# Other places, modulo 256 bytes, for the high and low weight parts that TensorE loads

## The chip, the cores and the metric

The kernel runs on one core of one Trainium2 chip. The metric is device time in microseconds (us), from start to end of one execution. An execution of the kernel before takes 3118.19 us, the median of two (3118.02 and 3118.37).

## What is computed

The reference is a block in float32 over one sequence of 256 tokens with 2048 features, followed by a second kind of block, which is applied twice. Each takes a normed input through wide projections, a few attention heads or a recurrence, gates and an output projection:

```python
h = rms_norm(x, g);  proj = h @ w_in            # 2048 x 17408, then twice 2048 x 16192
y_rnn  = (rg_lru(rnn_x) * silu(rnn_gate)) @ w_rnn_out
y_attn = (dilated_attention(q, k, v) * silu(attn_gate)) @ w_attn_out
x = x + rms_norm((sigmoid(g_rnn) * y_rnn + sigmoid(g_attn) * y_attn) @ w_o, ln_post_g)
for l in range(2):                              # three attention branches A, B, C
    u = rms_norm(x, g_pre[l]) @ w_in2[l]
    y = sum(sigmoid(gate_n) * ((branch_n * silu(z_n)) @ w_branch[l, n]) for n in "ABC")
    x = x + y @ w_out2[l]
```

Nearly all the arithmetic is multiplication of a 256-token activation matrix by weight matrices that are each used once.

## The kernel before

**Two parts of every number.** TensorE multiplies in a one-pass type (`fp32r`) that keeps fewer bits than float32. So each weight and each activation is held as a high part (a rounded copy) and a low part (what the rounding lost), and three of the four products are summed: high by high, high by low, low by high. ScalarE makes the high parts (`hi`, line 929, its instruction is line 937), VectorE the low ones (`lo`, line 1275, its instruction is line 1280), both from the buffer `raw`, into which the SyncE queue loads the weights by DMA.

**Tiles.** Weights come in units of 8 row tiles by 256 columns (128 x 2048 numbers). Units go to two slots in turn (`j % 2`). A unit is made, freed and used by halves of 1024 columns (`h`). The buffer `hl` holds, for each slot, the high parts of both halves and the low parts of both halves. `part(j, e, h, ...)` (line 218) gives the columns of slot `j`, part `e` (0 high, 1 low), half `h`. Right behind `hl` in on-chip memory lies `hT` and behind it `uT`, the activations: for each of 16 row tiles 512 columns, 256 tokens in high parts and then the same 256 in low parts. `hT` begins 4 x `HL` bytes behind the start of `hl`, and `hT` and `uT` are each 32768 bytes a partition, a multiple of 256.

**The matrix multiplications.** Every one on `pg` is issued by `mm` (line 536) and has two operands: the stationary one (128 x 128), loaded by a LDWEIGHTS ahead of it, and the moving one, which streams past. In `feature_major` (line 562) the stationary operand is a weight tile from `hl` and activations move: the wide one (512 columns) multiplies high weights by high and low activations at once, the narrow one (256 columns) low weights by high activations. They alternate, wide, narrow, wide, narrow; where `SIDE` (line 98) says so, a row tile or a half has its wide ones first and then its narrow ones. A half is 8 wide and 8 narrow ones. In `token_major` (line 570, for the values of the attentions) the roles are swapped: an activation tile is stationary, and the weights of `hl` move, high and low parts as one operand of two stretches (`both_view`, line 582). `queries` (line 803) and `keys_and_values` (line 812) issue their three products as single narrow ones. Each stationary tile starts a multiple of 512 bytes from the start of its half, and each moving one of `feature_major` a multiple of 1024 bytes from the start of `hT` or `uT`, so that within a half all have the same place modulo 256 bytes.

**Order.** TensorE's order is written out (`EVENTS`, `unit`). PSUM results are joined by ScalarE (line 945) and VectorE (line 1287). Small multiplications on `pa` for the attentions, the recurrence and the norms, most of them in plain float32, stand between the halves.

Of the kernel before, what the change touches and what calls it, by code (L numbers as in the profile page):

```python
# [26 lines left out]
UC = 2048  # L27
# [120 lines left out]
RAW_CHUNKS, RAW_HEAD = 5, 6  # L148


HI_AT, LO_AT, SLOT, HL = 16, UC + 32, 2 * UC + 128, 4 * UC + 224


PRE_SUMS = [1, 2 + NCH, 4 + 2 * NCH]
# [33 lines left out]
def build(nc, xT, w_in, w_gate, w_rnn, w_att, w_o, w_in2, w_uq, w_ukv, w_br, w_out2,  # L188
          vec1, vec2, blam, consts, tabs, bias_c, outT):
    ctx = ExitStack()  # L190
    with ctx:
        def sb(name, cols, dt=F32):
            return ctx.enter_context(nc.sbuf_tensor(name, [P, cols], dt))
# [5 lines left out]
        hl = sb("hl", HL, F32R)  # L199
# [17 lines left out]

        def part(j, e, h, a=0, n=UC // 2):

            first = j % 2 * SLOT + (LO_AT if e else HI_AT) + h * UC // 2 + a  # L220
            return hl[:, first:first + n]

        h3 = hT[:, :].rearrange("p (t n) -> p t n", n=512)
# [151 lines left out]
        def _(sp):  # L375
# [62 lines left out]
            with sp.Fori(0, PAIRS) as p:  # L438
                u = U_P1 + p * units("1")
                for part, base in enumerate((Q1, K1, V1)):  # L440
                    for g in range(3):
                        for j in range(2):
                            wide(u + 6 * part + 2 * g + j, j, w_in, base + 1024 * g + p * CH, 1024 * j)
                for j in range(2):
                    wide(u + 18 + j, j, w_in, Z1 + p * CH, 1024 * j)
                for j in range(4):
                    wide(u + 20 + j, j, w_in, G_ATT + (2 * p + j // 2) * CH, 1024 * (j % 2))
# [86 lines left out]
        def _(pe):  # L534
# [3 lines left out]
            def split_view(j, n):  # L538

                return [[part(j, e, k * n // (UC // 2), k * n % (UC // 2), n) for k in range(UC // n)] for e in range(2)]  # L540
# [37 lines left out]
            def apart_view(j, n):  # L578

                return [[part(j, e, h, 0, n) for h in range(2)] for e in range(2)]  # L580

            def both_view(j, n):
                views = []
                for k in range(UC // n):
                    h, a = k * n // (UC // 2), k * n % (UC // 2)
                    first = j % 2 * SLOT + HI_AT
                    pair = hl[:, first:first + 2 * (LO_AT - HI_AT)].rearrange("p (e n) -> p e n", e=2)
                    views.append(pair[:, :, h * UC // 2 + a:h * UC // 2 + a + n])
                return views

            def opening(u0, c0, tiles_ready, first_parts, weights_parts=None, summed=None):
# [20 lines left out]
            def unit(u, j, c, cj, op, first, last, form="f", subs=2, ready=None, halves=(0, 1), first_parts=None, side=()):  # L612

                base = 0 if first else 8
                if form == "k":
                    base, first, last = 0, True, True
                wh, wl = split_view(j, CH)
                if form == "r":
                    wh, wl = ([[w[h][:, k * P:k * P + P] for k in range(4)] for h in range(2)] for w in apart_view(j, 512))
                for h in halves:  # L620
                    pe.wait_ge(lo_done, 2 * u + h + 5)
                    if first and h == 0 and c is not None:
                        pe.wait_ge(evac_done, c + 1)
                    start, stop = first and h == 0, last and h == 1
                    parts = [range(base + 4 * h, base + 4 * h + 4)] if form != "k" or h == 0 else [(4, 5), (6, 7)]
                    if first_parts is not None and h == 0:
                        parts = first_parts
                    for n, ks in enumerate(parts):
                        if ready is not None:
                            ready(ks)  # L630
                        b, begin, end = 2 * (cj % 2), start and n == 0, stop and n == len(parts) - 1
                        if form == "r":
                            ins = feature_major(b, subs, wh[h], wl[h], op, ks, begin, end, base + 4 * h, side)
                        elif form == "t":
                            ins = token_major(b, wh, both_view(j, CH), op, ks, begin, end, base, side)
                        else:
                            ins = feature_major(b, subs, wh, wl, op, ks, begin, end, base, side)
                    ins.then_inc(half_done, 1)
# [253 lines left out]
            for l in range(2):  # L892
# [20 lines left out]
                for kind in "ABC":  # L913
                    turns = 2 if kind == "A" else 1
                    with pe.Fori(0, PAIRS // turns) as i:
                        for n in range(turns):
                            p = i * turns + n
# [1034 lines left out]
```

## Time and profile before

| | |
|---|---|
| median of the runs | 3118.19 us |
| the profiled execution's own time, its span | 3120.9 us, 3119.0 us |
| TensorE matmul busy | 3097.6 us (99%), 18230 instructions |
| TensorE weight load busy | 2731.5 us (88%) |
| VectorE, ScalarE busy | 2128.8 us (68%), 1733.3 us (56%) |
| DMA engines, mean busy share | 59.4% for the one data queue |
| granted TensorE clock | 0.998 of full speed |

The span runs from the first to the last instruction; the execution's own time also holds what lies around it. A matmul's busy time includes the flow through the array, which overlaps the next one. So the distance from one start to the next says more than the busy time: where a run of n matmuls is one row, it is (length of the row less the length of the last) / (n - 1).

### The profile page before, as it was taken

Reading aid. Unit: us, or ns where it says so; the run is one execution under the profiler, and the core shown is the slowest. Engines: PE = TensorE matmul, PEld = TensorE weight load, DVE = VectorE, ACT = ScalarE, POOL = GpSimd, SP = SyncE. Lnnn points to the kernel's source line nnn. Section 1 sums busy time; section 2 is a strip of 40 time slices with the busy share of each in tenths; the row PEclk is TensorE's granted clock in tenths of the full one; section 3 lists DMA queues with packets and bytes.
Section 4 is the critical chain, followed back from the end, with each engine's and each line's share of the span. In section 5 each row is a group of like instructions: output and inputs, shape, how many; then the busy total and the mean of one; then the engine's idle time right before and its main releaser. Section 6 shows DMA issues by size and latency. Waiting matters only on the chain.

```text
span 3119.0 us, 52176 instructions
## 1 busy us (share of the span) xinstructions
PE 3097.6 (99%) x18230; PEld 2731.5 (88%) x18230; DVE 2128.8 (68%) x2741; ACT 1733.3 (56%) x2291; POOL 0.2 (0%) x4
## 2 busy tenths in 40 slices
PE   9999999999999999999999999999999999999999
PEld 7888888888888788888888888888988888888888
DVE  7677576666667687767676565777776767656574
ACT  5685444444445556656565555645665656555563
POOL 0000000000000000000000000000000000000000
PEclk9999999999999999999999999999999999999999
DMA  7656655555556565565656665666556565666555
GB/s 228 194 176 197 205 189 167 184 180 174 183 169 211 179 174 161 160 204 171 182 167 195 192 185 176 189 197 185 160 160 205 170 182 167 195 192 186 176 187 175
DMA packets 569810, 571.67 MB, mean 183 GB/s; under 512 B 26353, under 2 KB 565489, under 8 KB 569713
## 3 DMA queue, kind: packets, MB, share of 16 engines
q1 hardware_dynamic: 569712, 570.42, 59.4%
q8 instruction: 56, 0.92, 0.1%
q14 instruction: 42, 0.34, 0.0%
HBM read 568.25 MB, written 2.10 MB: 183 GB/s over the span
## 4 chain that ended last, share of the span: by engine, by line
PE 96%; DVE 2%; ACT 1%; issue 1%; DMA 0%; SPq 0%; DVEq 0%; ACTq 0%
PE pg L536 90%; PE pa L775 1%; PE pa L792 1%; PE pa L782 1%; PE pa L536 1%; PE pa L751 1%; DVE hl L1280 1%; PE pa L793 1%; ACT hl L937 0%; PE pa L708 0%; PE pa L883 0%; DMA raw<-w_in 0%; DVE mix L1815 0%; DVE xres L1739 0%; DVE uT L1818 0%
## 5 line engine op out<-in xcount | busy, mean ns | idle before, releaser
L536 PE MATMUL pg<-hT,hl 128*128 128x512 f32 x11456 | 2001.4, 335 | 1.2 <-DVE hl L1280 1.1
L536 PEld LDWEIGHTS pg<-hT,hl 128*128 128x128 f32 x11456 | 1732.9, 188 | 235.0 <-DVE hl L1280 5.4
L1280 DVE TENSOR_TENSOR hl<-raw,hl 128x1024 fp32r<-128x1024 f32 (+1 forms) x1071 | 1255.1, 1210 | 299.6 <-ACT hl L937 291.9
L937 ACT ACTIVATE hl<-raw 128x1024 fp32r<-128x1024 f32 (+1 forms) x1071 | 1085.1, 1044 | 295.1 <-PE pg L536 277.9
L536 PE MATMUL pg<-uT,hl 128*128 128x256 f32 (+1 forms) x3712 | 631.5, 332 | 15.9 <-DVE uT L1361 7.4
L536 PEld LDWEIGHTS pg<-uT,hl 128*128 128x128 f32 x3712 | 555.8, 190 | 87.0 <-issue 15.5
L945 ACT ACTIVATE corr<-pg 128x512 f32<-128x512 f32 x286 | 170.2, 595 | 822.8 <-PE pg L536 822.8
L536 PE MATMUL pg<-hl,hT 128*128 128x512 f32 (+1 forms) x1792 | 318.5, 336 | 0.0
L536 PEld LDWEIGHTS pg<-hl,hT 128*128 128x128 f32 x1792 | 274.6, 188 | 38.6
L1287 DVE TENSOR_TENSOR work<-pg,corr 128x512 f32<-128x512 f32 (+1 forms) x154 | 105.8, 687 | 293.6 <-ACT corr L945 293.3
L1112 ACT ACTIVATE work<-work,sm 128x256 f32<-128x256 f32 (+3 forms) x144 | 69.3, 482 | 131.1 <-DVE sm L1558 129.1
L1287 DVE TENSOR_TENSOR gat<-pg,corr 128x512 f32 (+1 forms) x71 | 49.0, 690 | 133.0 <-ACT corr L945 133.0
L1287 DVE TENSOR_TENSOR xres<-pg,corr 128x512 f32<-128x512 f32 x32 | 22.1, 691 | 42.1 <-ACT corr L945 42.1
L1558 DVE TENSOR_REDUCE sm<-work 128x1 f32<-128x256 f32 (+3 forms) x144 | 49.0, 391 | 1.9
L1118 ACT ACTIVATE uT<-work 128x256 f32 x52 | 20.0, 414 | 53.2 <-DVE work L1689 53.2
L984 ACT ACTIVATE work<-pa,sm 128x256 f32<-128x256 f32 (+1 forms) x58 | 42.1, 726 | 3.4 <-PE pa L693 2.2
L1567 DVE RECIPROCAL sm<-sm 128x2 f32<-128x2 f32 (+1 forms) x56 | 9.5, 170 | 50.3 <-ACT work L1112 50.3
L1554 DVE SCALAR_TENSOR_TENSOR work<-pa,tab 128x384 f32<-128x384 f32 (+2 forms) x56 | 43.6, 779 | 0.0
L1287 DVE TENSOR_TENSOR corr<-pg,corr 128x512 f32<-128x512 f32 x15 | 10.4, 691 | 48.5 <-ACT corr L945 48.5
L792 PE MATMUL pa<-work 128*128 128x256 f32 x144 | 42.8, 378 | 0.0
L985 ACT ACTIVATE work<-work 128x256 f32<-128x256 f32 (+1 forms) x58 | 39.7, 685 | 1.8
L980 ACT ACT_TABLE_LOAD x31 | 39.8, 1283 | 1.3 <-PEq L1946 0.7
(191 smaller groups left out, 1369.1 us busy)
## 6 DMA issues: line engine op xcount, KB each, us to landing
raw<-w_in SPq DMA_DIRECT2D x791, 512.0 KB, 4.7
raw<-w_br SPq DMA_DIRECT2D x96, 512.0 KB, 4.3
raw<-w_out SPq DMA_DIRECT2D x64, 512.0 KB, 4.8
raw<-w_rnn SPq DMA_DIRECT2D x32, 512.0 KB, 4.9
raw<-w_o SPq DMA_DIRECT2D x32, 512.0 KB, 5.3
raw<-w_att SPq DMA_DIRECT2D x16, 512.0 KB, 4.7
raw<-w_uq SPq DMA_DIRECT2D x16, 384.0 KB, 3.9
tab<-tabs SPq DMA_DIRECT2D x5, 896.0 KB, 7.3
```

Of the source, the lines that this page charges most:

```text
L536: return nc.tensor.matmul(out, lhsT, rhs, start=start, stop=stop, skip_group_check=True)
L792: nc.tensor.matmul(weighted(kind, e), va, pt[:, 0:S], start=m == 0, stop=False, skip_group_check=True)
L937: nc.scalar.activation(part(j, 0, h, 0, n), raw[:, bass.ds(j % 2 * UC + a, n)], ACT.Copy)\
L945: nc.scalar.activation(cr[:, cj % 2, 0:n, :], pg3[:, b:b + n, S:], ACT.Copy)\
L980: act.preload_act_table_set("natural_log_exp_and_others")
L984: steps.done(nc.scalar.activation(out, mean, ACT.Ln, bias=eps, scale=scale))
L985: ins = nc.scalar.activation(out, out, ACT.Exp, scale=-0.5)
L1112: ins = nc.scalar.activation(part, part, ACT.Exp, bias=nmax[:, n:n + 1], accum_out=lsum[:, n:n + 1])
L1280: tt(part(j, 1, h, 0, n), raw[:, bass.ds(j % 2 * UC + a, n)], part(j, 0, h, 0, n).bitcast(F32), ALU.subtract).then_inc(lo_done, 1)
L1287: return tt(out, pg3[:, b:b + n, 0:S], cr[:, cj % 2, 0:n, :], ALU.add)
L1554: steps.done(stt(sc.rearrange("p (m n) -> p m n", m=nm), pa3[:, bank:bank + nm, 0:SM], SCALE[kind], tab[:, m0:m0 + SM * nm].rearrange("p ( ...
L1558: ins = nc.vector.tensor_reduce(nmax[:, n:n + 1], part, AX.XY if kind == "1" else AX.X, ALU.max, negate=True)
```

## The change

Four constants go (`HI_AT`, `LO_AT`, `SLOT` and the old `HL`), and a table `AT[slot][part][half]` takes their place, which gives the first column of each of the eight pieces of `hl`. Nothing else is touched: the same instructions on the same numbers, in the same order, with the same waits. Before, both halves and both slots had one place for high parts and one for low parts modulo 256 bytes; now each slot and half has a pair of its own. `hl` grows from 8416 to 8624 columns of 4 bytes, so that `hT` and all that lies behind it moves up by 832 bytes.

```diff
-HI_AT, LO_AT, SLOT, HL = 16, UC + 32, 2 * UC + 128, 4 * UC + 224
+AT = (((48, 2160), (1120, 3216)), ((4288, 6400), (5344, 7472)))
+HL = 8624
...
         def part(j, e, h, a=0, n=UC // 2):
 
-            first = j % 2 * SLOT + (LO_AT if e else HI_AT) + h * UC // 2 + a
+            first = AT[j % 2][e][h] + a
             return hl[:, first:first + n]
...
                 for k in range(UC // n):
                     h, a = k * n // (UC // 2), k * n % (UC // 2)
-                    first = j % 2 * SLOT + HI_AT
-                    pair = hl[:, first:first + 2 * (LO_AT - HI_AT)].rearrange("p (e n) -> p e n", e=2)
-                    views.append(pair[:, :, h * UC // 2 + a:h * UC // 2 + a + n])
+                    first, apart = AT[j % 2][0][h], AT[j % 2][1][h] - AT[j % 2][0][h]
+                    pair = hl[:, first:first + 2 * apart].rearrange("p (e n) -> p e n", e=2)
+                    views.append(pair[:, :, a:a + n])
                 return views
```

## Rows read from the trace of the kernel before

**Rows 1.** The page's first lines: busy time by engine, and its chain by engine.
```profile
span 3119.0 us, 52176 instructions
...
PE 3097.6 (99%) x18230; PEld 2731.5 (88%) x18230; DVE 2128.8 (68%) x2741; ACT 1733.3 (56%) x2291; POOL 0.2 (0%) x4
...
PE 96%; DVE 2%; ACT 1%; issue 1%; DMA 0%; SPq 0%; DVEq 0%; ACTq 0%
```

**Rows 2.** Waits of TensorE: engine, line, releaser, us in total, times, longest.
```profile
PE pg L536 <- DVE uT L1361: 7.4, 3, 3.7
PE pg L536 <- DVE hl L1485: 6.8, 1, 6.8
PE pg L536 <- DVE hl L1280: 1.9, 5, 0.5
```

**Rows 3.** Groups by line and shape, whole span (out<-moving,stationary): busy us, mean ns | idle us.
```profile
L536 PE MATMUL pg<-hT,hl 128*128 128x512 f32 x5728 | 1969.6, 393 | 1.2 <-DVE hl L1280 1.1
L536 PE MATMUL pg<-hT,hl 128*128 128x256 f32 x5728 | 1560.4, 277 | 0.0
L536 PE MATMUL pg<-uT,hl 128*128 128x512 f32 x1664 | 574.9, 395 | 15.9 <-DVE uT L1361 7.4 <-DVE hl L1485 6.8 <-DVE hl L1280 0.8
L536 PE MATMUL pg<-uT,hl 128*128 128x256 f32 x2048 | 504.9, 280 | 0.0
L536 PE MATMUL pg<-hl,hT 128*128 128x512 f32 x896 | 312.4, 393 | 0.0
```

**Rows 4.** Windows: stretch, its us, TensorE busy us (matmuls), granted clock, DMA share, GB/s.
```profile
251.00:442.00 191.00, 191.00 (x1126) 1.00 0.64 202
583.57:605.77 22.20, 22.20 (x130) 1.00 0.62 198
```

**Rows 5.** Timeline in four short windows, matmuls and weight loads: start us, length us.
```profile
1300.03 0.50 PE L536 MATMUL pg<-hT,hl 128*128 128x512 f32 x2
...
1300.26 0.50 PE L536 MATMUL pg<-hT,hl 128*128 128x256 f32 x2
...
1300.26 0.19 PEld L536 LDWEIGHTS pg<-hT,hl 128*128 128x128 f32 x1
...
122.16 3.61 PE L708 MATMUL pa<-xres 128*128 128x256 f32 x16
```

**Rows 6.** Timeline, runs of one kind of one-pass matmul.
```profile
246.70 1.55 PE L536 MATMUL pg<-hT,hl 128*128 128x512 f32 x6
...
248.43 1.00 PE L536 MATMUL pg<-hT,hl 128*128 128x256 f32 x7
...
1174.86 3.58 PE L536 MATMUL pg<-uT,hl 128*128 128x256 f32 x29
```

**Rows 7.** The chain that ended last, in order of time: start us, length us, what.
```profile
1715.90 0.93 PE pa L536 x4
...
1753.02 32.80 PE pg L536 x192
...
1956.64 5.48 PE pg L536 x32
```

**Rows 8.** Groups by line and shape: the two instructions that write the weight parts.
```profile
L1280 DVE TENSOR_TENSOR hl<-raw,hl 128x1024 fp32r<-128x1024 f32 x1047 | 1239.7, 1222 | 296.2 <-ACT hl L937 288.5
...
L937 ACT ACTIVATE hl<-raw 128x1024 fp32r<-128x1024 f32 x1047 | 1071.0, 1054 | 284.7 <-PE pg L536 267.5 <-DMA raw<-w_in 9.9 <-DMA raw<-w_o 3.5
```

## The prediction, made before the changed kernel was run

> **What bounds the kernel now.** I read the busy times and the chain first: TensorE's matmuls cover 99% of the span and 96% of the chain [rows 1]. The waits come next: few have a name, and the longest sums are 7.4, 6.8 and 1.9 us [rows 2]. So the time is the number of matmuls times the distance between their starts, and the change can only act on that distance. The groups by shape give the numbers [rows 3]: 5728 + 1664 = 7392 wide feature-major matmuls, each with a narrow partner (2048 - 1664 = 384 narrow ones are left, in the products of branch A), and 896 token-major pairs.
>
> The distance is in the windows [rows 4]. From 251 to 442 us nothing but alternating wide and narrow ones run, at full clock: 191.00 us for 1126 matmuls, one or two of which began before the window, so 562 pairs at 191.00 / 562 = **340 ns a pair**. That is 17/16 of 768 columns at 2.4 GHz (320 ns). The token-major stretch from 583.57 to 605.77 holds 64 pairs of its own, besides a row at each edge: 22.20 / 64 = **346.9 ns a pair**. The columns and the clock are the same. What differs is which buffer moves and which is loaded, and with it the place of the one relative to the other.
>
> **Who meets whom.** A weight load begins with a matmul: at 1300.26 both a narrow matmul and a load start [rows 5]. So while matmul i streams its moving operand, the stationary tile of matmul i+1 is being read. During a wide one low weights are loaded, during a narrow one high weights. What counts is then (place of the loaded tile - place of the moving one) modulo 256 bytes. I call it the lag.
>
> Before: high parts start at 16 x 4 = 64, low parts at 2080 x 4 = 128 (mod 256), half and slot add multiples of 256, and `hT` lies at 8416 x 4 = 128. Lags: low 0, high 64 - 128 = 192. Token-major: activations loaded at 128 while high weights move at 64, lag 64.
>
> After: `hT` lies at 8624 x 4 = 192. High parts: slot 0 at 192 in both halves, slot 1 at 0. Low parts: slot 0 at 128 and 64, slot 1 at 128 and 192. So the lags (high, low) become slot 0: (0, 192) and (0, 128); slot 1: (64, 192) and (64, 0). The change's title says (64, 0), (64, 192), (128, 0), (128, 64). Those differ from mine by 64 in both entries, because the longer `hl` moves the activations too. None is the old pair (192, 0).
>
> **The price of a lag, where the trace shows one.**
> - Wide, lag 192: the run of wide ones at 246.70, (1.55 - 0.39) / 5 = 232 ns [rows 6].
> - Wide, lag 0: four wide ones of the norm sums, moving and stationary both from `uT`, 0.93 / 4 = 232 ns [rows 7]. Lag 128 appears nowhere; between a wide one in step (2/3 of 340 = 227) and the 232 of its neighbours I take 232, the nearest rows out of step.
> - Narrow, lag 0: (1.00 - 0.28) / 6 = 120 ns, the run at 248.43 [rows 6].
> - Narrow, lag 192: from the products in threes of branch A, (3.58 - 0.28) / 28 = 118 ns on average over two loads of lag 192 and one of lag 0, so (3 x 118 - 120) / 2 = 117 [rows 6].
> - Pair with lag 64: the token-major 346.9.
>
> Added up, slot 0 would take 232 + 120 = 352 a pair and slot 1 about 347, mean 349.5. The same sum for the old places is 232 + 117 = 349, and the trace has 340: the alternating pair there falls into a rhythm in which both operands go by without loss, and lags alone don't foretell it. The lower end for each place is therefore 340, the upper end the sum. I put one of the four places in step, but with a re-entry at each half, since the lags now change every 2.7 us. What an entry costs: 32 matmuls behind small other work take 5.48 us against 16 x 0.34 = 5.44, so 40 ns, 5 ns a pair over the 8 pairs of a half [rows 7]. That place counts 345. The forecast is 0.75 x 349.5 + 0.25 x 345 = 348.4 ns.
>
> What the old kernel really has per pair in a mixed stretch: 32.80 / 96 = 341.7 ns [rows 7]. So each of the 7392 pairs pays 348.4 - 341.7 = 6.7 ns more: **+49 us**.
>
> **The other parts.** Token-major pairs: lags become 0 in slot 0 (load at 192, high weights moving at 192) and 192 in slot 1, by the prices above 352 and 349 instead of 346.9, about 3 ns x 896 = +3 us; bounds -6 us (340) and +5 us. The 384 single narrow ones read slot 0 (lags 0, and 192 or 128): at most 120 - 118 = 2 ns each, under 1 us. The writers of the parts, lines 1280 and 937, take 1.22 and 1.05 us a half [rows 8] and end inside the 2.72 us that TensorE needs for one; they cost nothing here, and without that cover a tenth more on 1047 of each would be 128 and 110 us. No slot, wait or DMA is added; a slower TensorE gives all others more time. The small multiplications on `pa` have both operands behind `hl` and keep their lags. The few stops of rows 2 stay.
>
> Sum: +49 + 3 = +52, less some because the sum of single prices overstated the old places by 9 ns, and the new ones may lie partly lower: I take **+47 us**. The profiled execution's 3120.9 becomes 3168; it stands 2.7 us over the median 3118.2, so the predicted time is **3165 us**.
>
> **A rule against this.** The rows show that the one-pass narrow matmul takes 113 to 120 ns while other operands differ in place alone. The Trainium skill says otherwise: "SBUF — State Buffer", section "Who interferes with whom", gives TensorE two independent read ports, one for the moving operand and one for LDWEIGHTS, and ends "PE and ACT never wait on anyone". By that rule places can't matter, and the time would stay 3118 us. The 340 against 346.9 of rows 4 speaks against it, though there the roles are swapped too and not the places alone; it is the first rival below.
>
> **The rivals.**
> 1. *No effect.* 17/16 may be what a one-pass stream takes whatever is loaded, and the token-major 7 ns may come from the swapped roles (two stretches in one operand). For it: 340 ns holds over 191 us without a slip. Against: single-kind runs of the same operands are slower (232 and 120, not 227 and 113). Then 3118, within 3110 to 3130.
> 2. *Slower by more, collision at every load.* If the changing lags keep TensorE from any rhythm: 232 + 120 = 352 for all, and the entry of 5 ns a pair on top, 357 - 341.7 = 15 ns x 7392 = +113 us, 3231 us. It decides from about 350 ns a pair on, where 2% is lost (62 us / 7392 = 8.4 ns a pair). For it: narrow, lag 0, is the dearest row, and all of slot 0 has it. Against: the old sum overstated.
> 3. *Faster: one place beats 17/16.* A plain float32 matmul of 256 columns has starts (3.61 - 0.38) / 15 = 215 ns apart [rows 5], near 512 columns' 213 at 2.4 GHz. If new places let one-pass ones run like this, a pair takes 215 + 108 = 323, up to 19 ns less; all four would give -138 us (2980), one of four -35 us (3083). For it: no row has lag 128. Against: no stretch in the trace, at any of three lags, goes below 340 a pair. By the Trainium skill's "TensorE: Matmul & The Clock Gate", section "Wait — 56ns, not 53.3ns?", starts are N / 2.4 GHz + 2.5 ns apart, 325 for a pair; the trace's 340 doesn't agree for this type.
> 4. *It doesn't do what it says*: if the title's pairs were the true lags (activations unmoved), slot 0 would have narrow 64 and slot 1 narrow 128, unpriced; by the sums above +30 us, inside the forecast.
>
> **How the numbers follow.** A change of 2% is 62 us, about what can be told from none. Forecast, with rival 4 in it (3130 to 3200): 0.63, of which I put 0.16 above 3181. No effect: 0.17. Slower by more: 0.14. Faster: 0.06, of which over 2% only where two places or more gain, 0.02. So slower by over 2% 0.16 + 0.14 = 0.30, faster by over 2% 0.02, within 0.68. The range takes the no-effect case and most of the forecast up to the foot of rival 2: 3114 to 3214.
>
> **What would show it.** In the changed profile the window 251:442 should hold about 1100 matmuls, not 1126, and not one stretch of 191 us in one rhythm; slot 0's halves should be longer than slot 1's, because of narrow ones of 120 ns; the runs on `pa` should keep 0.93 us for four; DVE and ACT instruction lengths and the waits should not move. Wrong would be: all halves at 2.72 us (rival 1), pairs under 340 (rival 3), or a named wait of TensorE that grew.

## The result: 3166 us, and the profile after

The changed kernel takes 3166.11 us (median of two, 3165.81 to 3166.42) against 3118.19: a ratio of 1.0152, 95% interval 1.0136 to 1.0168, **+48 us** where +47 was forecast. The page of the changed kernel (busy time by engine, chain by engine) has the same engines in the same order as [rows 1], each share within one point; TensorE's busy time has grown by 44 us with no instruction more:

```profile
span 3164.5 us, 52176 instructions
...
PE 3141.8 (99%) x18230; PEld 2751.5 (87%) x18230; DVE 2130.0 (67%) x2741; ACT 1733.0 (55%) x2291; POOL 0.2 (0%) x4
...
PE 97%; DVE 1%; ACT 1%; DMA 0%; SPq 0%; issue 0%; ACTq 0%; DVEq 0%
```

TensorE's waits (line numbers are one higher throughout) are those of [rows 2], with 2.2 us more on low parts:

```profile
PE pg L537 <- DVE uT L1362: 7.9, 3, 3.5
PE pg L537 <- DVE hl L1486: 6.7, 1, 6.7
PE pg L537 <- DVE hl L1281: 4.1, 6, 1.6
```

The writers of the parts, against [rows 8], have not moved by more than 1 ns:

```profile
L1281 DVE TENSOR_TENSOR hl<-raw,hl 128x1024 fp32r<-128x1024 f32 x1047 | 1240.4, 1221 | 315.4 <-ACT hl L938 307.9
...
L938 ACT ACTIVATE hl<-raw 128x1024 fp32r<-128x1024 f32 x1047 | 1070.2, 1053 | 307.2 <-PE pg L537 288.1 <-DMA raw<-w_in 9.7 <-DMA raw<-w_o 4.4
```

So the time is in the distance between matmuls. The two windows of [rows 4], in the changed kernel:

```profile
251.00:442.00 191.00, 191.00 (x1099) 1.00 0.61 196
583.57:605.77 22.20, 22.20 (x129) 1.00 0.60 189
```

1099 instead of 1126 in the same 191 us at the same clock. Counted as the prediction counts, less the two that may have begun before the window, these are 548.5 pairs of 191.00 / 548.5 = 348.2 ns where it was 340. (The second window begins at another point of the work.) The chain of the changed kernel in order of time (start, length, what), for [rows 7]:

```profile
1743.95 0.92 PE pa L537 x4
...
1769.13 5.54 PE pg L537 x32
...
1781.57 33.40 PE pg L537 x192
```

33.40 / 96 = 347.9 ns a pair where it was 341.7: 6.2 x 7392 = 46 of the 48 us. The four wide ones on `pa`, whose two operands moved together, stay at 0.92 us.

The 96 pairs of this row are not all of one kind: by their tiles, 80 are feature-major and the last 16 token-major. Taking 346.9 ns for each of the 16 in both, the 80 took (32.80 - 5.55) / 80 = 340.6 ns before and take (33.40 - 5.55) / 80 = 348.1 now, 7.5 ns more, and in the long window the step is 8.2 ns. At that price 7392 pairs would cost 55 to 61 us and not 48. Part of the rest is that the kernel before was not in step everywhere. A later window, in the kernel before and then in the changed one:

```profile
2000.00:2100.00 100.00, 100.00 (x574) 1.00 0.61 190
```

```profile
2000.00:2100.00 100.00, 100.00 (x576) 1.00 0.58 184
```

100.00 / 286 = 350 ns a pair before the change, at the old lags and at full clock; the changed kernel is a little quicker here. In the trace of the kernel before, 326 pairs in a row from 1995.8 us and 270 from 3020.3 us run like this.

The four places show in four halves in a row, timeline of the changed kernel. Each row runs from a half's third matmul to its fifteenth, wide at both ends, so a pair is (length - 0.395) / 6:

```profile
304.55 2.48 PE L537 MATMUL pg<-uT,hl 128*128 128x512 f32 x13
...
307.33 2.49 PE L537 MATMUL pg<-uT,hl 128*128 128x512 f32 x13
...
310.14 2.52 PE L537 MATMUL pg<-uT,hl 128*128 128x512 f32 x13
...
312.97 2.43 PE L537 MATMUL pg<-uT,hl 128*128 128x512 f32 x13
```

Slot 0 with lags (high, low) = (0, 192) takes 347 ns and with (0, 128) 349; slot 1 with (64, 192) takes 354 and with (64, 0) 339, which is in step. From the first start of a half to the first of the next, entries included, they are 347, 351, 353 and 342, mean 348.3. The mean is the forecast's, the places are not: the dearest half was to be in slot 0.

### The profile page after: what moved, and what is told of

Its sections match the earlier page's. It is cut to its first block, busy times and chain, and to the rows that moved or that the text cites. A ratio compares the mean times of both kernels' runs of the same rounds, so it can differ in the third digit from the quotient of the medians.

```text
span 3164.5 us, 52176 instructions
## 1 busy us (share of the span) xinstructions
PE 3141.8 (99%) x18230; PEld 2751.5 (87%) x18230; DVE 2130.0 (67%) x2741; ACT 1733.0 (55%) x2291; POOL 0.2 (0%) x4
## 4 chain that ended last, share of the span: by engine, by line
PE 97%; DVE 1%; ACT 1%; DMA 0%; SPq 0%; issue 0%; ACTq 0%; DVEq 0%
PE pg L537 91%; PE pa L776 1%; PE pa L793 1%; PE pa L537 1%; PE pa L783 1%; PE pa L752 1%; PE pa L794 1%; DVE hl L1281 0%; PE pa L709 0%; DMA raw<-w_o 0%; PE pa L884 0%; DMA raw<-w_in 0%; ACT hl L938 0%; SPq L456 0%; DVE uT L1362 0%
## 5 line engine op out<-in xcount | busy, mean ns | idle before, releaser
L537 PE MATMUL pg<-hT,hl 128*128 128x512 f32 x11456 | 2036.4, 338 | 2.1 <-DVE hl L1281 2.0
L537 PE MATMUL pg<-uT,hl 128*128 128x256 f32 (+1 forms) x3712 | 639.4, 334 | 16.8 <-DVE uT L1362 7.9
```

Of the source, the lines that this page charges most:

```text
L537: return nc.tensor.matmul(out, lhsT, rhs, start=start, stop=stop, skip_group_check=True)
```

## The experiments

Four theories. **L**: the lags set the distance. **A**: the absolute place in memory does, or the longer `hl`. **C**: only lags that change from half to half cost. **M**, formed after the first four kernels: L with memory, that is, the same pair of lags has more than one rhythm, and what ran before picks it. Ratios are against the kernel before, with 95% intervals.

**All lags alone, TensorE alone (grid).** The edit replaces the block by one line for each pair of lags:

```python
run((192, 0), mm)      # 64 pairs: for k in 8, s in 2: wide(k, s), narrow(k, s), four times
```

> A program of its own, in place of the block: after one load and two copies, TensorE alone runs 31 stretches of 64 wide and 64 narrow one-pass matmuls (or 64 of one kind), each stretch with a fixed pair of lags (high, low): all 16 pairs of 0, 64, 128, 192, four single wide, four single narrow, and seven with lags of 16 or 32 bytes between. Theory L (the lag of the loaded tile to the moving one sets the distance): (192, 0) takes 340 ns a pair, (64, 192) 341, (64, 0) 347, (0, 192) 350, (0, 128) 352 to 353, as in the kernels; at least one other pair reaches 340, none goes below. Rival A (the place in memory itself, or what the other engines do at the time, sets it): all 16 pairs take the same here, 340. Rival C (only the change of lags from half to half costs): all 16 settle at 340 as well.

Its chain in order of time; each line of the program is one pair of lags (high, low). L73 is (0, 128), L74 (0, 192), L75 (64, 0), L78 (64, 192), L79 (128, 0), L80 (128, 64), L83 (192, 0), L86 (192, 192); L87, L89 and L90 are wide ones only, lag 0, 128 and 192, L91 and L94 narrow ones only, lag 0 and 192:

```profile
64.85 22.19 PE pg L73 x128
87.04 22.40 PE pg L74 x128
109.44 21.78 PE pg L75 x128
...
176.22 22.59 PE pg L78 x128
198.81 22.52 PE pg L79 x128
221.33 22.19 PE pg L80 x128
...
288.17 21.76 PE pg L83 x128
...
354.31 22.61 PE pg L86 x128
376.92 14.51 PE pg L87 x64
...
406.36 14.88 PE pg L89 x64
421.24 14.65 PE pg L90 x64
435.89 7.67 PE pg L91 x64
...
458.69 7.54 PE pg L94 x64
```

Divided by 64: (64, 0) and (192, 0) take 340 ns a pair, (0, 128) and (128, 64) 347, (0, 192) 350, (128, 0) 352, (64, 192) and (192, 192) 353. Seven of the eight not shown lie between 347 and 353; (0, 0), which ran first and began with wide ones 427 ns apart and more, settles at 347. No pair goes under 340. Nothing else runs here, and the spread is that of the kernels: A and C, which had all at 340, fall. Single kinds: wide 227 at lag 0, 233 at 128, 229 at 192; narrow 120 at lag 0, 118 at 192. Of the pairs off the grid, (192, 16) also took 340 and (176, 0), (208, 0), (192, 32) 347 to 353.

**Same lags, other absolute places (shift_all).**

```diff
-HI_AT, LO_AT, SLOT, HL = 16, UC + 32, 2 * UC + 128, 4 * UC + 224
+HI_AT, LO_AT, SLOT, HL = 32, UC + 48, 2 * UC + 128, 4 * UC + 240
```

> The kernel before with weight parts and activations all 64 bytes further on, so that all lags stay (192, 0). Theory L: 3118 us, 340 ns a pair between 251 and 442 us. Rival A (the place in memory itself counts, modulo 256): off 3118 by tens of us, as the changed kernel is. Rival C: 3118.

Measured: ratio 1.0002 (0.9992 to 1.0011); the first window holds x1125. Moving every place by the same 64 bytes costs nothing that can be seen; more places of the moving tile are in grid2.

**One pair of lags everywhere (uni_64_192, uni_0_128).**

```diff
-AT = (((48, 2160), (1120, 3216)), ((4288, 6400), (5344, 7472)))
+AT = (((0, 2112), (1056, 3168)), ((4224, 6336), (5280, 7392)))      # uni_64_192
+AT = (((48, 2160), (1104, 3216)), ((4272, 6384), (5328, 7440)))      # uni_0_128
```

> The changed kernel with one pair of lags for all slots and halves, (64, 192), that of its fastest place (slot 1, first half, 227 + 114 ns once settled). Theory L: 341 ns a pair throughout, the entry cost of each half gone: 3118 to 3130 us. Rival A: near the changed kernel's 3166, as hl is as long and the activations lie where they lie there. Rival C: 3118.

> The changed kernel with one pair of lags for all, (0, 128), that of its slowest place (slot 0, second half, 352 to 353 ns). Theory L: (352.5 - 341.7) x 7392 = +80 us, about 3198 us. Rival C (only lags that change from half to half cost): 3118. Rival A: 3166.

Both expectations took the halves of the changed kernel one off: the in-step half is (64, 0), and (64, 192) is the dearest. The numbers of the grid are what counts, and they hold. uni_64_192 came out at 3201.69 us, ratio 1.0268 (1.0251 to 1.0285), uni_0_128 at 3161.32 us, 1.0139 (1.0122 to 1.0156). The chain of the one, then of the other, at the stretch of 96 pairs of [rows 7]:

```profile
1799.81 33.92 PE pg L537 x192
```

```profile
1777.51 33.35 PE pg L537 x192
```

353.3 and 347.4 ns a pair, the 16 token-major ones included; less 341.7, times 7392, that is +86 and +42 us, measured +83 and +42. C falls a second time: lags that never change cost as much.

**The old lags in the new layout (uni_192_0).**

```diff
-AT = (((48, 2160), (1120, 3216)), ((4288, 6400), (5344, 7472)))
+AT = (((32, 2144), (1072, 3184)), ((4256, 6368), (5296, 7408)))
```

> The changed kernel, its longer hl and moved activations kept, with the old lags (192, 0) in all slots and halves. Theory M: 3118 us, all of the +48 gone. If any of it is owed to the longer hl, to the strides of the two-part operand or to what ScalarE and VectorE meet at the new places, as much of it stays.

Ratio 1.0006 (0.9996 to 1.0015). The +48 us are the lags; what the rest of the new layout costs is within that interval, at most 5 us.

**The other pair that took 340 (uni_64_0).**

```diff
-AT = (((48, 2160), (1120, 3216)), ((4288, 6400), (5344, 7472)))
+AT = (((0, 2112), (1072, 3184)), ((4224, 6336), (5296, 7408)))
```

> The changed kernel with lags (64, 0) in all slots and halves, the other pair that took 340 in the grid. Theory L: 3118 us, within 10, 340 ns a pair between 251 and 442 us; whether it is a little under the kernel before hangs on how soon it gets back into step behind other work. Rival C: 3118. Rival A: near 3166.

A miss, and the one that made theory M: 3168.05 us, ratio 1.0160 (1.0146 to 1.0174). The chain of uni_64_0 at the same stretch:

```profile
1783.01 33.56 PE pg L537 x192
```

349.6 ns a pair, and 350 for the 80 feature-major ones, with the very lags that took 340 alone.

**Entry, narrower loads, places of the moving tile (grid2).** The same program with `run([(0, 192)], mm, times=1, ks=4)` and so on in the kernel's order, then stationary tiles cut with `m=64`, `m=32`.

> A second program of TensorE alone, in place of the block. First the four lag pairs of the changed kernel in its own order, 8 wide and 8 narrow matmuls each: (0, 192), (0, 128), (64, 192), (64, 0), eight times round. Theory L with memory (the lags set the distance, but which rhythm a pair of lags falls into depends on what ran before): 347, 350, 353 and 340 ns a pair as in the changed kernel, though (0, 192) alone took 351 and (0, 128) alone 348. Theory L without memory: 351, 348, 354, 340. Then (0, 192) alone after (192, 0) and after (64, 0). Then stationary tiles of 64 and of 32 columns instead of 128: if the reading of the load gets in the way of the moving one, the bad pairs (64, 192), (192, 192), (128, 0) come down from 353 towards 340 with fewer columns to load; if 17/16 itself is owed to the loads, (192, 0) falls under 340. If the lag acts in another way, nothing changes. Last (192, 0) and (64, 192) with the moving tile itself at 0, 128, 192, 96 and 32 bytes (modulo 256): theory L 340 and 354 for each; rival A differs.

Its chain. L68 to L71 are (0, 192), (0, 128), (64, 192), (64, 0) in turn, a half each; L73 is (0, 192) after (192, 0). L77 and L78 are (64, 192) and (192, 192) with 64 columns loaded, L80 is (192, 0) with 32. L86 and L87 are narrow ones alone, lag 0, with 64 and 32 columns. L89 is (64, 192) at another place of the moving tile:

```profile
119.47 2.77 PE pg L68 x16
122.24 2.81 PE pg L69 x16
125.05 2.83 PE pg L70 x16
127.88 2.74 PE pg L71 x16
...
152.38 22.19 PE pg L73 x128
...
240.28 22.18 PE pg L77 x128
262.45 21.98 PE pg L78 x128
...
306.80 22.05 PE pg L80 x128
...
410.50 7.26 PE pg L86 x64
417.75 7.25 PE pg L87 x64
...
446.79 22.60 PE pg L89 x128
```

The first four, over 8: 346, 351, 354 and 342 (the last with its entry), as in the changed kernel. (0, 192) takes 347 here and took 350 in the first program, behind another pair. With 64 columns loaded (64, 192) and (192, 192) fall from 353 to 347 and 343, and the narrow matmul at lag 0 from 120 to 113: the width of the load bears on the distance. That reading the load is what gets in the way is a guess from this, and not shown: the edit also narrows the output to 64 rows, (128, 0) falls only from 352 to 350, with 32 columns (64, 192) and (192, 192) are back at 349 and 348, and (192, 0) goes up to 345. And 113 for 256 columns, 17/16, stays with half and with a quarter of the load; no run had no load at all. (64, 192) took 353 at all five places of the moving tile, (192, 0) 340.

**The lags of the title (title).**

```diff
-HL = 8624
+HL = 8608
```

> The changed kernel with hl 16 columns shorter (8608), which puts the activations back and gives the lags of the title: (64, 0), (64, 192) in slot 0, (128, 0), (128, 64) in slot 1. Theory L, by the grid's 340, 354, 353 and 348, mean 348.6 against 341.7: +51 us, 3170 us, and slot 0's first half in step. Rival A (absolute places, which stay those of the changed kernel for all of hl): the halves as in the changed kernel.

3177.64 us, ratio 1.0191 (1.0175 to 1.0206): +59 us against +51 expected. 96 pairs take 33.58 us (350 ns), and (64, 0) takes 349, out of step. The forecast's rival 4 had +30 for it. The edit moves the activations and leaves all of `hl` where it is, and the time changes by 11 us: it is the place of the one relative to the other that counts.

**Two pairs that can be in step (two_rhythms).**

```diff
-AT = (((48, 2160), (1120, 3216)), ((4288, 6400), (5344, 7472)))
+AT = (((32, 2144), (1072, 3184)), ((4224, 6336), (5296, 7408)))
```

> The changed kernel with lags (192, 0) in slot 0 and (64, 0) in slot 1, both in step by the grid but not the same. It tells what the change of lags costs by itself: theory L, 16 ns at each entry into (64, 0) as the grid's first matmuls show, 462 pairs of halves, +7 us, 3126. Rival C (the change from half to half is what costs): a good part of the changed kernel's +48.

3132.29 us, ratio 1.0047 (1.0031 to 1.0062), +13 us; in the first window x1125, as good as before. The rest is in stretches behind stops, where 96 pairs take 33.57 us instead of 32.80. Changing lags is nearly free while both stay in step.

**Six orders, and what a stop does (grid3).**

```python
for r in range(8):                      # one of the six orders, a half each
    run([(0, 192)], mm, times=1, ks=4); run([(64, 192)], mm, times=1, ks=4)
    run([(0, 128)], mm, times=1, ks=4); run([(64, 0)], mm, times=1, ks=4)
```

> A third program of TensorE alone, in place of the block. First the four lag pairs of the changed kernel in each of their six cyclic orders, eight times round. Theory M (lags set the distance, with memory of what ran before): (192, 0) and (64, 192) take the same in every order; (64, 0) is in step (340 ns a pair) only in some orders, that after (64, 192) among them, and takes 347 to 350 in others; (0, 192) and (0, 128) move between 347 and 351. So the mean over the four changes with the order by some ns. Theory L without memory: every order has the same mean. Then, each behind four plain float32 matmuls, single lag pairs: (64, 0) takes 349 to 350 as in the kernel with (64, 0) everywhere, (192, 0) 340, (64, 192) 354.

The chain of the third program. L78 to L81 are the four pairs of lags in the order (0, 192), (64, 192), (0, 128), (64, 0); L98 and L101 are plain float32 matmuls, L99 is (64, 0) behind them, L102 (192, 0):

```profile
299.89 2.82 PE pg L78 x16
302.71 2.80 PE pg L79 x16
305.51 2.78 PE pg L80 x16
308.30 2.80 PE pg L81 x16
...
580.59 11.31 PE pg L99 x64
...
593.62 11.20 PE pg L102 x64
```

In this order the four take 352, 350, 348 and 350; (64, 0) isn't in step, and (64, 192) isn't the dearest. (64, 0) is in step, 342 with its entry, in the four orders in which (0, 192) or (64, 192) runs just before it, and takes 350 in the two in which (0, 128) does. The means of the six orders run from 347.9 to 350.0; M holds, except that (64, 192), which M as I wrote it had constant, moves too (350 to 353). The stop is the surprise: behind it even (192, 0) takes 11.20 / 32 = 350 ns a pair and stays there for all 32 pairs, and (64, 0) takes 11.31 / 32 = 353.

**That order in the kernel (other_order).**

```diff
-AT = (((48, 2160), (1120, 3216)), ((4288, 6400), (5344, 7472)))
+AT = (((48, 2176), (1120, 3232)), ((4272, 6400), (5328, 7472)))
```

> The changed kernel with the same four lag pairs dealt out in another order: slot 0 has (0, 192) and (64, 192), slot 1 has (0, 128) and (64, 0). In the third program of TensorE alone this order took 352, 350, 348 and 350 ns a pair, mean 350.0, and that of the changed kernel 348.3, with (64, 0) no more in step. Theory M: (350.0 - 348.3) x 7392 = +13 us over the changed kernel, 3179 us, (64, 0) halves at 349 instead of 340. Theory L without memory: 3166, as the four pairs are the same.

3176.94 us, ratio 1.0186 (1.0169 to 1.0203), against 3179 expected and 3166 without memory. Its chain at the 96 pairs:

```profile
1786.50 33.58 PE pg L537 x192
```

**The order of wide and narrow behind a stop (no_side).**

```diff
+SIDE = {"RX": {}, "RG": {}, "1": {}, "A": {1: (), 3: (), 4: (), 5: ()}, "B": {}, "C": {}, "head": [{}, {}]}
```

> The kernel before with the table SIDE emptied: after a stop a half starts with wide, narrow, wide, narrow at once, no longer with two or more wide ones first; lags stay (192, 0). In the third program (192, 0) behind plain float32 matmuls and in this order stayed out of step, 118 + 232 = 350 ns. Theory M: the halves behind small multiplications stay out of step until the next stop; if half of the 7392 pairs do, +37 us, 3155 us; 3118 if other stops bring the rhythm back. New waits for low parts, which SIDE covers, can add some us. Theory L without memory: 3118 plus those waits, all pairs at 340.

3132.32 us, ratio 1.0048 (1.0031 to 1.0065): +14 us, less than expected, since most stretches find the rhythm all the same (the 96 pairs take 32.79 us). Where they don't, they stay out to the next stop. The chain of the kernel before, then of no_side, at the same 288 pairs:

```profile
507.56 98.38 PE pg L536 x576
```

```profile
505.93 100.59 PE pg L537 x576
```

98.38 and 100.59 us, the same in three of the four passes of that loop: 6.6 of the 14 us. (The fourth goes over into other work and has no such row.) 64 of the 288 pairs are token-major; at 346.9 ns each in both, the other 224 go from 340 to 350. The waits by name grew by 2.4 us.

No version beat the kernel before; no lags in the grid offer a pair under 340 ns.

## Why the prediction was right

- *TensorE's distance is the time; nothing else moves.* Right in the main: counts, the writers of the parts and the clock as before, and uni_192_0 gives back all 48 us. One thing that was to be a sign of being wrong did show, a named wait that grew: 4.1 us on low parts for 1.9. uni_192_0 has 3.2 there and no lost time, so it is no part of the cause.
- *The lag and not the absolute place; the activations move too, so the title's numbers aren't the lags.* Right: shift_all 1.0002; the title's lags cost 59 us, not 48.
- *The old pair is in a rhythm that the new ones mostly miss; one place in four in step.* It came true in count, and nearly in price: 342 ns with its entry, where 345 was taken. But no row stood behind the count, and which place, (64, 0), was not named. That is luck: in other_order the same four pairs of lags have none in step.
- *The prices per lag, added.* This step was weak. Wide at lag 0 was priced at 232, from norm sums behind other work; alone it takes 227. Wide at lag 128 was priced at 232 with no row, and takes 233 alone. By the sums slot 0 was 352 and slot 1 347; measured are 347 and 349 for slot 0, 354 and 339 for slot 1. Errors of 3 to 8 ns a place cancelled in the mean: 349.5 x 0.75 + 345 x 0.25 = 348.4 against 347.9. That +47 met +48 is partly luck. What is not: out-of-step pairs, with 128 columns loaded, lie between 346 and 354 in every program here, so with one place in step any such prices would have given +21 to +69 us (an estimate: means of 344.5 to 351.0, less 341.7, times 7392), and with none up to +91.
- *"What the old kernel really has per pair in a mixed stretch", 341.7.* Misread: 16 of those 96 pairs are token-major, and the feature-major ones took 340.6 there. As the base for all 7392 it is right all the same, since some 600 of them ran at 350 elsewhere, which the forecast did not look for; over the whole trace, alternating feature-major pairs are 341.6 ns long on average before and 348.2 after. Two slips that cancelled.
- *"Slot 0's halves should be longer than slot 1's".* Wrong: the longest are in slot 1, (64, 192).
- *Entry cost of 40 ns a half.* Too high: 240 and 116 ns instead of 227 and 113 at the first pair, 16 ns.
- *Token-major +3 us.* Not resolved; its mean matmul is 394 ns long against 393, about 1 us in all.
- *The rivals.* No effect, with the rule of the Trainium skill behind it ("SBUF — State Buffer", "Who interferes with whom": TensorE's two read ports are independent, "PE and ACT never wait on anyone"), falls: with nothing else at work, the same pairs of matmuls take 340 to 353 ns by their lags alone. Collision at every load falls in the mean, though with (64, 192) everywhere the kernel comes near it: 353 ns a pair and +83 us. Faster falls: none of the 16 pairs, and no narrower load, went under 17/16. The 325 ns a pair that the Trainium skill's "TensorE: Matmul & The Clock Gate", section "Wait — 56ns, not 53.3ns?", gives, at N / 2.4 GHz + 2.5 ns for each matmul, are not reached by any of them.

Open is how the two streams make each other wait. The runs show that the lag and the width of the load matter, and that there are several stable rhythms; no run shows the mechanism.

## What to carry to other kernels

Where TensorE is fed back to back with a fresh stationary tile for each one-pass float32 matmul, the place of the loaded tile relative to the moving one, modulo 256 bytes, was worth up to 4% here (340 to 354 ns a pair), and growing a buffer in front of the activations changes it. Measure pairs of lags in the kernel's own order and behind its stops, not one by one: a pair that is best alone need not be so there: (64, 0) takes 340 alone and (0, 128) 347, but everywhere in the kernel (64, 0) gives 3168 us and (0, 128) 3161. Divide a stretch's length by its pairs before and after any change of layout; busy shares and waits don't show it. Do so in several stretches: at its old lags too this kernel has two long ones at 350 ns a pair. Back at 340, their 596 pairs would give about 6 us (an estimate from 596 x 10 ns).

## What the runs showed of the hardware that was not expected

- The same instructions at the same lags have more than one lasting rhythm: (64, 0) 340 or 350 ns a pair, and 353 behind plain float32 matmuls, (0, 192) 347 or 350, (192, 0) 340 or, behind plain float32 matmuls and starting wide, narrow, 350.
- Two wide ones first behind a stop (`SIDE`) brought (192, 0) back into step in the loop of four passes (98.38 against 100.59 us for 288 pairs).
- A rhythm can also be lost with no other work between: in the kernel before, two starts at 1995.18 and 1995.37 us lie 0.19 us apart where a narrow one had taken 0.11, and the 326 pairs behind them run at 350 ns instead of 340, at the same lags.
- A one-pass float32 stream of 256 or 512 columns never ran under 17/16 of a cycle a column at 2.4 GHz in any stretch (113.3 and 226.7 ns), while plain float32 ones of 256 columns were 215 ns apart, near 512 cycles.
